# Spreading the running sums by DMA in a two-block transformer kernel, with new PSUM banks for the z tiles and a reordered end

## The reference, cut to what matters

```
def step(state, inp):                                # Mamba-2 scan, 32 heads in 4 groups
    cum = jnp.cumsum(dt_c * A_g, axis=1)             # running sums
    seg = cum[:, :, None] - cum[:, None, :]
    L = jnp.exp(jnp.where(causal, seg, -jnp.inf))    # decays
    CB = jnp.einsum('btgn,bsgn->btsg', C_c, B_c)
    y_intra = jnp.einsum('btsg,btsgh,bsgh,bsghp->btghp', CB, L, dt_c, x_c)
...
    x = x + 0.5 * swiglu(rmsnorm(x, ffn2_norm[l]), ffn2_w_in[l], ffn2_w_out[l])
return rmsnorm(x, final_norm)                        # over the 1024 channels of a token
```

## Time and profile before

| what | value |
|---|---|
| median of 3 runs | 1819.04 us (1818.71 to 1819.98) |
| profiled execution, its own time | 1818.82 us |
| its span | 1817.0 us |
| around the span (1818.82 - 1817.0) | 1.82 us |
| TensorE busy | 1805.2 us, 99% |
| VectorE busy | 1040.9 us, 57% |
| ScalarE busy | 726.3 us, 40% |
| GpSimd busy | 46.9 us, 3% |

### The profile page before, as it was taken

The page is one execution under the profiler, slowest core; times in us unless marked ns, Lnnn a source line. Parts: engine busy times, 40 slices in busy tenths (PEclk is TensorE's granted clock), DMA queues, the critical chain, the costliest instruction groups (busy, mean ns, idle before and its releaser), DMA issues.

```text
span 1817.0 us, 21253 instructions
## 1 busy us (share of the span) xinstructions
PE 1805.2 (99%) x8416; PEld 1460.3 (80%) x8416; DVE 1040.9 (57%) x1512; ACT 726.3 (40%) x1198; POOL 46.9 (3%) x107
## 2 busy tenths in 40 slices
PE   9999999999999999999999999999999999999998
PEld 7777777888766788888888888888888888888887
DVE  8899886566688475444333356654444544444334
ACT  5787775343377533232222343223222322322221
POOL 1001011000210000000000000000000000000000
PEclk9999999999999999999999999999999999999999
DMA  5222222222211223333333423233333333333331
GB/s 180 70 70 73 76 69 85 92 96 89 74 42 36 71 83 102 104 94 93 96 96 100 127 73 102 93 94 103 93 96 101 93 94 104 93 93 99 99 96 56
DMA packets 48195, 163.44 MB, mean 90 GB/s; under 512 B 5345, under 2 KB 7777, under 8 KB 48097
## 3 DMA queue, kind: packets, MB, share of 16 engines
q1 hardware_dynamic: 47088, 161.24, 28.5%
q10 hardware_dynamic: 1008, 0.85, 0.1%
HBM read 159.97 MB, written 2.10 MB: 89 GB/s over the span
## 4 chain that ended last, share of the span: by engine, by line
PE 97%; DVE 2%; ACT 0%; issue 0%; DMA 0%; DVEq 0%; SPq 0%; ACTq 0%
PE pb L749 29%; PE pb L751 28%; PE pb L750 28%; PE pb L860 2%; PE pb L970 2%; PE pb L999 1%; PE pb L975 1%; PE pb L1129 1%; PE pb L1131 1%; PE pb L1130 1%; PE pb L763 1%; PE pb L812 0%; PE pb L833 0%; PE pb L819 0%; PE pb L1139 0%; PE pb L773 0%
## 5 line engine op out<-in xcount | busy, mean ns | idle before, releaser
L749 PE MATMUL pb<-XR,wr 128*128 128x512 f32 x1584 | 625.3, 395 | 0.6 <-DVE wl L1521 0.5
L751 PE MATMUL pb<-XR,wl 128*128 128x512 f32 x1584 | 616.9, 389 | 0.0
L750 PE MATMUL pb<-XL,wr 128*128 128x512 f32 x1584 | 616.9, 389 | 0.0
L1521 DVE TENSOR_TENSOR wl<-raw,wr 128x1024 fp32r<-128x1024 f32 (+1 forms) x297 | 358.2, 1206 | 350.8 <-ACT wr L1187 349.7
L1187 ACT ACTIVATE wr<-raw 128x1024 fp32r<-128x1024 f32 (+1 forms) x295 | 305.4, 1035 | 302.4 <-PE pb L751 276.9
L749 PEld LDWEIGHTS pb<-XR,wr 128*128 128x128 f32 x1584 | 297.4, 188 | 65.6 <-issue 3.9
L751 PEld LDWEIGHTS pb<-XR,wl 128*128 128x128 f32 x1584 | 297.4, 188 | 62.7
L750 PEld LDWEIGHTS pb<-XL,wr 128*128 128x128 f32 x1584 | 297.6, 188 | 60.2 <-issue 0.2
L749 PE MATMUL pb<-ffn2HR,wr 128*128 128x512 f32 (+1 forms) x198 | 72.5, 366 | 0.0
L750 PE MATMUL pb<-ffn2HL,wr 128*128 128x512 f32 (+1 forms) x198 | 72.3, 365 | 0.0
L751 PE MATMUL pb<-ffn2HR,wl 128*128 128x512 f32 (+1 forms) x198 | 72.3, 365 | 0.0
(11 more groups left out here) (339 smaller groups left out, 2255.1 us busy)
## 6 DMA issues: line engine op xcount, KB each, us to landing
raw<-in_ffn_in SPq DMA_DIRECT2D x88, 512.0 KB, 3.5
raw<-in_mix_in SPq DMA_DIRECT2D x48, 512.0 KB, 3.5
raw<-in_ssm_in SPq DMA_DIRECT2D x40, 512.0 KB, 3.3
raw<-in_ffn_out SPq DMA_DIRECT2D x32, 512.0 KB, 3.5
raw<-in_ffn_out SPq DMA_DIRECT2D x16, 384.0 KB, 3.1
raw<-in_mla_in SPq DMA_DIRECT2D x11, 512.0 KB, 3.3
raw<-in_ssm_out_a SPq DMA_DIRECT2D x8, 512.0 KB, 3.2
raw<-in_ssm_out_b SPq DMA_DIRECT2D x8, 512.0 KB, 3.3
```

The source lines that it names most:

```text
L749: e.matmul(o, r, xr, start=first, stop=False)
L750: e.matmul(o, r, xl, start=False, stop=False)
L751: return e.matmul(o, l, xr, start=False, stop=last)
L1521: e.tensor_tensor(wl[j % NS][:, 0:width(j)], raw[j % NR][:, 0:width(j)], wr[j % NS][:, 0:width(j)].bitcast(F32), ALU.subtract).then_inc(s_ ...
```

## The change

The change has four parts.

1. The running sums `CM` are written once to a tensor `cum` in device memory. From pair q = 2 on (28 heads) SP spreads a head's row over the partitions by a DMA into `DB[h % 2]` in SBUF, where ScalarE's `decays` reads it. The matmuls of these heads are gone. Heads 0 to 3 stay on TensorE.
2. `tok` 3 moves from tile 14 (step 7) to tile 15 (step 3).
3. From channel unit 33 on, the tiles use the banks 1, 0, 4, 5 in place of 1, 0. The last two z tiles (14 and 15) use 1, 0.
4. At the end, the sums of `ACC` run ahead (`early_sums`). The square moves to VectorE, and ScalarE's square root with one Newton step replaces three Newton steps. All eight scalings of the first half come ahead of the second half's residual. Channels 0 and 1 of the second half get their gain from ScalarE early and their row factor from GpSimd.

```
-            side.append((2 if x[1][0] == "gscale" else 7, x[1]))
+            side.append((2 if x[1][0] == "gscale" else 3 if x[1] == ("tok", 3) else 7, x[1]))
...
-    due += [(10, ("tok", 1)), (12, ("tok", 2)), (14, ("tok", 3))]
+    due += [(10, ("tok", 1)), (12, ("tok", 2)), (15, ("tok", 3))]
...
             if n == 33:
+                ring = Ring([1, 0, 4, 5])
+            if n == 14:
                 ring = Ring([1, 0])
...
+        def spread_decay(h):
+            if h == 4:
+                w.wait_ge(s_cumout, 16)
+                w.wait_ge(s_nct, 1)
+                w.wait_ge(s_chl, 1)
+            if h >= 6:
+                w.wait_ge(s_ll, h - 1)
+            e.dma_start(DB[h % 2][:, :].rearrange("p (a b) -> p a b", a=4),
+                        cum[:, :, h, :].to_broadcast([128, 4, 128])).then_inc(s_db[h % 2], 16)
+        two = {unit["ssm_in", u[1]] + 5: q for q, u in enumerate(pair_units(), 1)}
...
+            if two.get(j, 15) < 14:
+                spread_decay(2 * two[j] + 4)
+                spread_decay(2 * two[j] + 5)
...
-                elif what == "decay":
-                    decays(n)
...
+        def early_sums(p):
+            o = opened(("sum", p))
+            w.wait_ge(s_fold, sq.folded["fin", 6])
+            for i in (2 * p, 2 * p + 1):
+                m = e.matmul(o[:, 4 + i:5 + i], ACC[:, 128 * i:128 * i + 128], ones[:, 0:1], start=True, stop=True)
+            m.then_inc(s_presum, 1)
...
-                o = PB[bk.bank["decay", h]]
-                w.wait_ge(*bk.full["decay", h])
+                if q < 2:
+                    o = PB[bk.bank["decay", h]]
+                    w.wait_ge(*bk.full["decay", h])
+                else:
+                    o = DB[h % 2]
+                    w.wait_ge(s_db[h % 2], 16 * (q - 1))
...
+            e.activation(SS[:, k], SV[:, k], ACT.Sqrt).then_inc(s_lastroot, 1)
...
+        early_sum(0)
         last_residual(0)
         last_root(0)
-        last_scale(0, range(5))
+        last_scale(0, range(KT))
+        early_sum(1)
         last_residual(1)
-        last_scale(0, range(5, KT))
         last_root(1)
-        last_scale(1, range(KT))
+        last_scale(1, range(len(POOL_OUT), KT))
...
+        for i, n in enumerate(POOL_OUT):
+            e.tensor_tensor(H[:, n, 256:512], H[:, n, 256:512], RS[:, 256:512], ALU.mult).then_inc(s_poolfin, 1)
```

More of the change, by code:

```diff
@@ L373, in build_in @@
     prior = low("prior", [128, 1], F32, ph2)
+    DB = [low("DB1", [128, S], F32, ph2)]
+    ph3 = ExitStack()
+    DT, T1, T2, T3 = [low(n, [128, 128], F32, ph3) for n in ("DT", "T1", "T2", "T3")]
+    ph3.close()
+    DB = [low("DB0", [128, S], F32, ph2)] + DB
     ph2.close()
@@ L457, in build_in @@
     s_flip, s_nct, s_cmt = sem("s_flip"), sem("s_nct"), sem("s_cmt")
+    s_cumout, s_db = sem("s_cumout"), [sem(f"s_db{i}") for i in range(2)]
     s_u, s_conv, s_silu = sem("s_u"), sem("s_conv"), sem("s_silu")
@@ L657, in place_ffn @@
                 bk.place(("last", p), ring.next(), (s_last, p + 1), (s_res, 40 + p))
+                if p == 1:
+                    bk.place("row", ring.next(), (s_row, 1), (s_lastrow, 1))
                 b = 3 if p == 0 else ring.next()
                 bk.place(("sum", p), b, (s_sums, sums_no[f"fin{p}"]), (s_sv, taken[f"fin{p}"]))
-                bk.place(("spread", p), b, (s_spread, spreads[f"fin{p}"] + 1), (s_fin, 8 * p + 8))
+                bk.place(("spread", p), b, (s_spread, spreads[f"fin{p}"] + 1), (s_fin, KT))
     place_ffn(0)
@@ L722, in _ @@
             tk = slice(256 * p, 256 * p + 256)
[L723 to L726, removed]
+            for n in range(KT) if p == 0 else range(2, KT, 2):
+                w.wait_ge(s_fin, n + 1 if p == 0 else KT + n - len(POOL_OUT) + 1)
+                e.dma_start(out[n][:, tk], H[:, n, tk]).then_inc(s_out, 16)
+                if p == 1 and n >= 4:
+                    i = n // 2 - 2
+                    w.wait_ge(s_poolfin, i + 1)
+                    e.dma_start(out[POOL_OUT[i]][:, tk], H[:, POOL_OUT[i], tk]).then_inc(s_out, 16)
         w.wait_ge(s_out, 32 * KT)
@@ L1092, in last_spread @@
             m.then_inc(s_spread, 1)
+            if p == 1:
+                o = opened("row")
+                for i in (2, 3):
+                    m = e.transpose(o[:, 128 * i:128 * i + 128], RN[:, i:i + 1].to_broadcast([128, 128]), ident[:, :])
+                m.then_inc(s_row, 1)
         def last_tile():
@@ L1490, in _, with last_root @@
         ffn(1, None)
-        for p in range(2):
-            tk = slice(256 * p, 256 * p + 256)
-            w.wait_ge(s_res, 40 + p)
-            e.activation(TB[:, tk], H[:, 7, tk], ACT.Square).then_inc(s_lastsq, 1)
-        for n in range(1, KT, 2):
-            w.wait_ge(s_fin, 8 + n + 1)
-            e.dma_start(out[n][:, 256:512], H[:, n, 256:512]).then_inc(s_out, 16)
+        def last_root(p):
+            k = slice(2 * p, 2 * p + 2)
+            w.wait_ge(s_sv, taken[f"fin{p}"])
+            e.activation(SS[:, k], SV[:, k], ACT.Sqrt).then_inc(s_lastroot, 1)
+        last_root(0)
+        tk = slice(256, 512)
+        for n in POOL_OUT:
+            w.wait_ge(s_fin, n + 1)
+            e.activation(H[:, n, tk], H[:, n, tk], ACT.Copy, scale=col("final_norm", n)).then_inc(s_prescale, 1)
+        last_root(1)
+        w.wait_ge(s_row, 1)
+        e.activation(RS[:, tk], PB[bk.bank["row"]][:, tk], ACT.Copy).then_inc(s_lastrow, 1)
+        for n in range(3, KT, 2):
+            w.wait_ge(s_fin, KT + n - len(POOL_OUT) + 1)
+            e.dma_start(out[n][:, tk], H[:, n, tk]).then_inc(s_out, 16)
     @block.vector
@@ L2167, in last_residual, with early_sum @@
                                    op0=ALU.mult, op1=ALU.add).then_inc(s_res, 1)
+            w.wait_ge(s_res, 40 + p)
+            e.tensor_tensor(TB[:, tk], H[:, 7, tk], H[:, 7, tk], ALU.mult).then_inc(s_lastsq, 1)
+        def early_sum(p):
+            k = slice(2 * p, 2 * p + 2)
+            w.wait_ge(s_presum, p + 1)
+            e.tensor_scalar(RT[:, k], PB[bk.bank["sum", p]][:, 4 + 2 * p:6 + 2 * p], 1.0 / D, EPS, ALU.mult,
+                            ALU.add).then_inc(c.up(), 1)
+            w.wait_ge(c.h, c.n)
         def last_root(p):
```

49 lines of the change are left out of this document (36 added, 13 removed).

## The result

The changed kernel takes 1824.88 us (median of 8 runs, 1823.79 to 1826.36). The kernel before takes 1819.06 (8 runs, 1818.71 to 1819.98). The ratio is 1.0032, with a 95% interval of 1.0021 to 1.0043, so the change makes the kernel 5.8 us slower. The prediction of 1818.4 was wrong, and its range, which ends at 1821.6, does not hold the result.

The account below looks back on a forecast made before the run. TensorE, busy 99% of the span, was taken as the bound. Terms: -6.58 + 1.41 + 4.8 + 1.9 - 2.1 = -0.6 us from 1818.82, so 1818.2, median 1818.4; 8-in-10 range 1815.2 to 1821.6.

Parts of the forecast that it names:

- the banks: Tiles get four banks in place of two; TensorE does not wait for these banks now, so 0.
- after the stall VectorE lies further ahead: Behind the wait at `tok` 4, VectorE would lie further ahead of TensorE than before; given with the banks' 0.
- a second stall behind the first: A further TensorE stall after the one at `tok` 4, counted among the slower outcomes, chance 0.05.
- the first stall: At `tok` 4, TensorE waits for VectorE's moved `XD` until 114.1 us, 4.8 us later; 1.41 us saved only lengthens the wait.
- The clock's direction: Behind the wait at `tok` 4, TensorE falls to half clock for at most 3.8 us, losing 1.9 us.
- The spreading matmuls: Mixer, pairs q = 2 to 15: 14 pairs at 0.47 us leave TensorE, 6.58 us less; 11 pairs, 5.17, after the stall.
- The transfers: Loads into `DB` land in 5.2 to 7.2 us, within 9.2 us, cost 0; rival that they set the pace, 1836, chance 0.05.
- ScalarE's reads of SBUF: ScalarE reads SBUF in place of PSUM; its idle time covers a few hundredths per instruction, so 0.
- The end: Behind the last tile: scalings done at R + 5.9, R the residual's start, gaining 2.1 us; rival of no gain, 1820.5, chance 0.09.
- the output transfers behind the last scaling stay as they are: At the program's end, the output transfers after the last scaling were taken as unchanged.

Follow-up runs that it names:

- the version without the stalls: Changed kernel with banks going 0, 1 from z tile 14 on and `tok` 3 back in tile 14: 1812.74 us, ratio 0.9966.
- the half runs: Changed kernel with banks 0, 1 from z tile 14, `tok` 3 back in tile 14, and transfers in eight 256-byte runs per partition: 1877.43 us.

## Why the prediction was wrong

**The failed step is the banks.** "TensorE does not wait for these banks now, so 0" is true of the kernel before and says nothing of the new order. The edit changes which bank each tile gets, and the sequence of banks over the tiles was not read. It puts tile 14 behind tile 13 in one bank. Mending that order alone brings the kernel to 1819.49, inside the range. A term put at 0 measured 5.4 us in the medians and 5.0 in the profile. The rest of the argument, that after the stall VectorE lies further ahead, was wrong at that place too: by 283 us VectorE was waiting 1.90 us for ScalarE. The prediction had a chance of 0.05 for a second stall behind the first and gave it neither a place nor a price.

**The mechanism of the first stall was right**, its place, its cause and its time (113.86 for 114.1). Undoing it gave 7.0 us between the profiled executions, 6.75 with the banks mended, and 8.5 in the medians, which take in a clock drop at the second stall. The sum of its terms was 1.41 + 4.8 + 1.9 = 8.1; undoing it also brings back a wait of 1.0 to 1.7 us for the Silu, which the prediction did not name.

**The clock's direction was right, its size was too small for this execution.** The term was 1.9 us for the first stall. The changed kernel's profile shows 6.3 us at half clock behind it, 3.1 us, and the kernel before with the moved turns alone has `y` 3 as slow (4.31 us). With the banks mended, the same wait cost 1.9. So the start of the program, from which the 1.9 was taken, gave the lower of the two costs seen. For the second stall there was no term, and it measured 1.7.

**The spreading matmuls** were worth what was said: 5.1 us between the two stalls for 11 pairs (forecast 5.17). Put together, the version without the stalls takes 1812.74, and the new end alone 1817.68, so the rest of the change is worth 4.9 us of the 6.58 when nothing is in its way but a wait of 1.0 us for the Silu.

**The transfers** were costed at nothing, and that held, but by luck. The landing was 9.0 us and not 5.2 to 7.2, against a limit first read as 9.2 and estimated at 10.5 to 11 from the half runs. "ScalarE would wait nowhere for `DB`" was wrong: it waited 3.0 us in four waits, beside TensorE's work. "I leave it at 0" for ScalarE's reads of SBUF missed by 0.5 us: the decays out of `DB` take that much longer per pair, and at the second stall the other engines waited for them.

**The end** followed its steps within 0.15 us up to the last scaling. What failed is "the output transfers behind the last scaling stay as they are": the span now ends 2.9 us behind it in place of 2.1, which takes 0.8 off the 2.1. Of this 0.3 is the issue of one more small output behind the others, and the rest is not placed.

**With the terms as measured** the sum comes out. The forecast's difference was -0.6. The banks add 5.0, the first stall with its clock 0.8 (7.5 for 6.7), the spreading matmuls behind it 0.1 (5.1 for 5.17), and the end 1.1 (-1.0 in the two profiled executions for -2.1): +6.4, the growth of the span.

## What to carry to other kernels

When an edit renumbers buffers, write down the buffer of each tile in a row and look for two neighbours in the same one. That nobody waits for a buffer now says nothing of a new order, and a ring that is started again in the middle must begin with the buffer that was not used last. A gain on the engine that sets the pace lasts only until the next place where another engine's chain is full. There it turns into waiting, and the wait can cost the clock on top. And an edit that moves work later to save a short wait needs the same reading as one that adds work: here it paid about 7 us to save at most 1.7.

## What the runs showed of the hardware

- Spreading one row over 128 partitions by DMA, 256 KB, lands in 3.6 us as runs of 2 KB, in 8.5 to 9.2 us as runs of 512 bytes, and in 15.5 us as runs of 256 bytes. Between the last two the time grows nearly with the number of runs.
- Such transfers delay others on the same queue. The 512 KB weight loads beside them landed in 3.3 us (median) without them, in 3.9, 8.1 and 14.6 us beside runs of 2 KB, 512 and 256 bytes.
- After a wait of 4.8 us TensorE worked at half clock for 6.3 us in one profiled execution and for 3.9 in another (losses 3.1 and 1.9 us). After a wait of 3.06 us it first went on at full clock for 1.5 us, and only then had 3.4 us at half (loss 1.7 us). After one of 1.50 us the clock stayed at 1.00.
- ScalarE makes decays out of the spread sums in SBUF less closely packed than out of a PSUM bank. One decay of 128 x 128 shows 387 ns from `DB` and 377 from a bank in the changed kernel, but four of them in a row advance by 1.17 us from `DB` and by 1.00 from a bank.
- Three small outputs that followed each other on one queue took 0.41 to 0.46 us each to issue.
